# A two-block transformer on one core: gate columns as three products of split parts, gate areas used twice in the expert stage, latent scaling moved

## The reference, cut to what matters

```python
# first block, a layer
x = x + merged @ w_out                       # mixer
x = x + memory_cross_attention(...)
aff = softmax(h @ w_router)                  # 16 experts
gates, idx = top_k(aff.T, cap=32)            # each expert picks 32 tokens
a, u = xs @ w_gate[e], xs @ w_up[e]          # 1024 x 1024 each
y = (silu(a) * u) @ w_down[e] * gates        # added back at idx
# second block, a layer
p = rmsnorm(h) @ w_in                        # its last 2048 columns are gate_a, gate_b
y_a = rwkv7_time_mix(...) @ w_out_rwkv       # a scan over the tokens, done in chunks of 32
y_b = mla(q_lat, kv_lat, k_pe, ...) @ w_out_mla   # q_lat, kv_lat: columns of p, RMS-normed
h = h + (sigmoid(gate_a) * y_a + sigmoid(gate_b) * y_b) @ w_out
h = h + conv_ffn(rmsnorm(h))
```

## Time and profile before

| | us |
|---|---|
| median of 3 runs | 2285.09 |
| range of the 3 runs | 2283.28 to 2287.34 |
| the profiled execution's own time | 2283.18 |
| its span, first to last instruction | 2281.0 |
| PE busy | 2050.3 |
| DVE busy | 872.1 |
| ACT busy | 700.5 |

### The profile page before, as it was taken

The page is one execution under the profiler, slowest core; times in us unless marked ns, Lnnn a source line. Parts: engine busy times, 40 slices in busy tenths (PEclk is TensorE's granted clock), DMA queues, the critical chain, the costliest instruction groups (busy, mean ns, idle before and its releaser), DMA issues.

```text
span 2281.0 us, 38226 instructions
## 1 busy us (share of the span) xinstructions
PE 2050.3 (90%) x16988; PEld 1379.4 (60%) x16988; DVE 872.1 (38%) x1262; ACT 700.5 (31%) x1005; POOL 40.6 (2%) x65
## 2 busy tenths in 40 slices
PE   8999978788779999987778789999999999989998
PEld 6887433333328887333333338565899885658996
DVE  6444111110006444111111127246577472365774
ACT  5544111111115453111111125213444452144443
POOL 1000000000001000000000000000000000000000
PEclk9999898888889998888888889999999999999999
DMA  8246899999996247899999995221754352216540
GB/s 320 93 153 274 329 429 428 429 428 428 429 419 224 74 185 306 358 429 429 428 428 428 429 408 203 77 76 37 236 186 162 131 200 77 71 43 223 185 176 19
DMA packets 139087, 592.28 MB, mean 260 GB/s; under 512 B 5680, under 2 KB 59136, under 8 KB 114384
## 3 DMA queue, kind: packets, MB, share of 16 engines
q1 hardware_dynamic: 137856, 586.67, 65.0%
q0 software_dynamic: 1104, 3.70, 0.4%
HBM read 589.30 MB, written 1.05 MB: 259 GB/s over the span
## 4 chain that ended last, share of the span: by engine, by line
PE 68%; DMA 24%; DVE 3%; issue 2%; ACT 1%; SPq 1%; DVEq 0%; POOLq 0%; ACTq 0%; POOL 0%
PE ps L574 33%; DMA ring<-in_w_up 24%; PE ps L1163 11%; PE ps L2144 5%; PE ps L1984 2%; PE ps L890 2%; PE ps L1130 2%; PE ps L2183 1%; PE ps L1184 1%; PE ps L591 1%; PE ps L989 1%; PE ps L1085 1%; PE ps L1065 1%; DVE ring_lo L550 1%; SPq L781 0%
## 5 line engine op out<-in xcount | busy, mean ns | idle before, releaser
L1163 PE MATMUL ps<-ring,area 128*32 128x512 f32 x1984 | 312.1, 714 | 129.4 <-DMA ring<-in_w_up 129.4
L550 DVE TENSOR_TENSOR ring_lo<-ring,slab_hi 128x2048 fp32r<-128x2048 f32 x136 | 311.4, 2292 | 223.6 <-ACT slab_hi L545 223.4
L545 ACT ACTIVATE slab_hi<-ring 128x2048 fp32r<-128x2048 f32 x136 | 260.0, 1913 | 283.0 <-PE ps L574 265.2
L1163 PEld LDWEIGHTS ps<-ring,area 128*32 128x32 f32 x1984 | 73.2, 128 | 332.6 <-issue 168.1
L574 PE MATMUL ps<-hT_hi,slab_hi 128*128 128x256 f32 x832 | 234.7, 282 | 3.0 <-DVE hT_lo L567 1.5
L574 PE MATMUL ps<-hT_lo,slab_hi 128*128 128x256 f32 x832 | 233.4, 281 | 0.0
L574 PE MATMUL ps<-hT_hi,ring_lo 128*128 128x256 f32 x832 | 232.6, 280 | 0.0
L1749 DVE TENSOR_TENSOR area<-ps,par 128x256 f32<-128x256 f32 x32 | 13.6, 425 | 493.1 <-PE ps L1130 493.1
L1399 ACT ACTIVATE area<-ps 128x512 f32<-128x512 f32 x32 | 19.1, 597 | 552.2 <-PE ps L1163 552.2
L1184 PE MATMUL ps<-ring,area 128*32 128x512 f32 x992 | 160.3, 804 | 29.8 <-DVE area L1769 29.8
L574 PEld LDWEIGHTS ps<-hT_hi,slab_hi 128*128 128x128 f32 x832 | 156.1, 188 | 4.2 <-issue 2.2
(11 more groups left out here) (374 smaller groups left out, 2978.8 us busy)
## 6 DMA issues: line engine op xcount, KB each, us to landing
ring<-in_w_up SPq DMA_DIRECT2D x64, 2048.0 KB, 20.3
ring<-in_w_down SPq DMA_DIRECT2D x62, 2048.0 KB, 21.8
ring<-in_w_gate SPq DMA_DIRECT2D x60, 2048.0 KB, 14.9
ring<-in_w_ffn_up SPq DMA_DIRECT2D x44, 1024.0 KB, 7.8
ring<-in_w_in SPq DMA_DIRECT2D x18, 2048.0 KB, 10.0
ring<-in_w_ffn_down SPq DMA_DIRECT2D x10, 2048.0 KB, 7.8
ring<-in_xattn_w_kv SPq DMA_DIRECT2D x8, 2048.0 KB, 16.9
ring<-in_w_in SPq DMA_DIRECT2D x10, 1024.0 KB, 12.1
```

Source lines behind the costliest of these rows:

```text
L545: return m.nc.scalar.activation(hi, whole, ACT.Copy)
L550: return m.nc.vector.tensor_tensor(lo, whole, hi, ALU.subtract)
L1163: ins = mm(ps[32 * g:32 * g + CAP, 1, :], m.tokT[:, k, :], gate_up[i][:, k % 4, (g % 2) * BANK:(g % 2 + 1) * BANK], start=k == 0, stop=k = ...
```

## The change

1. *Expert stage.* `m.first_gate` is used twice a layer: for expert 0 and then for expert 2. The first halves (rows 0 and 1 of the four) of expert 1's first w_up slab and of expert 2's first w_gate slab are issued as soon as PE has done k = 0 and 1 of expert 0 (`first_rows_used`), the second halves after slot 2 is freed. Expert 2's second w_gate slab follows expert 1's first w_down slab. Slot 3 is freed by the first matmul of `gather` in place of the first transpose behind it.
2. *Gates.* Gate slabs 2 and 3 (32 of 64 steps a layer) become `exact` products: the normed tokens and both slabs are split, five `high` on ACT and five `low` on DVE a layer, each 128x2048. The parts lie in slots 0 and 1, whose gate slabs are used up by then, in the slabs themselves and in a new area `gate_hi`. The order of these steps changes (four k of tile 0, four of tile 1, and so on). Some `GATE_FILLS` in the second half grow by a step, the rest shrinks from seven steps to two.
3. *Ring.* Slots 0 and 1 are freed only at the head of `tensor_mla`. The order of the loads becomes half of w_out (slot 2), w_out_mla, w_out_rwkv, the other half of w_out.
4. *Latent norm.* Its four DVE instructions move in front of the wait for `h_full` in `vector_rwkv`.
5. `Aak` moves into slot 5, AREA grows by 320 columns, `gpsimd_between` waits two experts longer.

```diff
@@ sync_first
-    into_slots(GATE_SLOTS, up_down, 1, 1, 3)
+    up, gate = GATE_SLOTS, m.first_gate
+    sp.wait_ge(*m.at("first_rows_used", l))
+    for rows, loaded in ((slice(0, 2), m.s("second_up_rows_loaded")), (slice(2, 4), m.landed[up])):
+        if rows.start:
+            ring_wait(m, sp, up, l * HELD1_LAYER[up] + 1 + HELD1[up])
+        sp.dma_start(slab(m, up, 4, D)[:, rows], expert("w_up", 1, 0)[:, rows]).then_inc(loaded, 16)
+        sp.dma_start(gate[:, 0][:, rows], expert("w_gate", 2, 0)[:, rows]).then_inc(m.s("third_gate_loaded"), 16)
+    ring_wait(m, sp, up + 1, l * HELD1_LAYER[up + 1] + 1 + HELD1[up + 1])
+    sp.dma_start(slab(m, up + 1, 4, D), expert("w_up", 1, 1)).then_inc(m.landed[up + 1], 16)
+    into_slots(up + 2, ("w_down",), 1, 1, 1)
+    sp.dma_start(gate[:, 1], expert("w_gate", 2, 1)).then_inc(m.s("third_gate_loaded"), 16)
+    into_slots(up, ("w_up",), 2, 2)
     last_down(2)
-    into_slots(0, ("w_gate",), 2, 1)
-    into_slots(GATE_SLOTS, up_down, 2, 2, 3)
-    into_slots(0, ("w_gate",), 3, 2)
+    into_slots(up + 2, ("w_down",), 2, 2, 1)
+    into_slots(0, ("w_gate",), 3, 1)
@@ tensor_experts
+                if behind_up and k == 0 and t == 0:
+                    ins.then_inc(m.free[3], 1)
...
+                if first and k == 1 and g == 3:
+                    ins.then_inc(s("first_rows_used"), 1)
...
-            if c == 0:
+            if last and c == 0:
                 ins.then_inc(m.free[3], 1)
@@ sync_second
+    whole(W_OUT2, "w_out_2", 0)
+    whole(W_OMLA, "w_out_mla_2", 0, k=4, n=D)
     whole(W_ORW, "w_out_rwkv_2", 0, k=4, n=D)
-    whole(W_OMLA, "w_out_mla_2", 0, k=4, n=D)
-    for j in range(2):
-        whole(W_OUT2 + j, "w_out_2", j * BANK)
+    whole(W_OUT2 + 1, "w_out_2", BANK)
@@ tensor_second
-    release.append(W_GATES + PAIRS - 1)
+    release.extend((W_GATES + PAIRS - 1, W_GATES, W_GATES + 1))
@@ _gate_fills
-                     ("whole", 2), ("fourth_wide", 3), ("eighth", 2), ("keys", 3), ("block", 2), ("block_wide", 2), ("cross", 2),
-                     ("close", 2), ("rows", 2), ("wu", 3), ("q", 2), ("g", 1), ("h", 4)):
+                     ("whole", 2), ("fourth_wide", 3), ("eighth", 2), ("keys", 4), ("block", 3), ("block_wide", 2), ("cross", 3),
+                     ("close", 2), ("rows", 3), ("wu", 4), ("q", 2), ("g", 1), ("h", 4)):
...
+EXACT_GATES = 2
+def gate_step(i):
+    j, r = i // (2 * KD), i % (2 * KD)
+    if j < EXACT_GATES:
+        return j, r // KD, r % KD
+    return j, r // 4 % 2, r // KD * 4 + r % 4
...
+def gate_half(m, j, h):
+    slot, half = PLAN2[W_GATES + j].slot, slice(h * (SLAB // 2), (h + 1) * (SLAB // 2))
+    room = m.ring_lo[:, PLAN2[W_GATES + 1].slot]
+    hi = m.gate_hi[:, :] if (j, h) in ((2, 0), (3, 1)) else room[:, 0:SLAB // 2] if j == 2 else room[:, SLAB // 2:]
+    return hi, m.ring_lo[:, slot, half], m.ring[:, slot, half]
@@ fill, in tensor_rwkv
+                if k % 4 == 0 and t == 0:
+                    wait("gate_lo", 2 * (j - EXACT_GATES) + k // 4 + 2)
...
+                first, ins = exact(m, out, rows, w, k == 0, k == KD - 1)
+                if j == PAIRS - 1 and k == 0 and t == 0:
+                    first.then_inc(used(W_GATES + j - 1), 1)
...
-            elif k == 0 and t == 0 and j:
-                ins.then_inc(used(W_GATES + j - 1), 1)
+            elif j == EXACT_GATES and t == 1 and k == 3:
+                ins.then_inc(s("gates_half"), 1)
@@ scalar_rwkv, behind block(1, "D2", 0)
+    wait("gates_full", 2)
+    wait("n1_whole")
+    high(m, *gate_rows_split(m)).then_inc(s("gate_hi"), 1)
+    landed2(m, act, l, W_GATES + 2)
+    high(m, *gate_half(m, 2, 0)).then_inc(s("gate_hi"), 1)
     gate_rows("second_wide")
     block(3, "D", 2)
     gate_rows("fourth_wide")
+    high(m, *gate_half(m, 2, 1)).then_inc(s("gate_hi"), 1)
+    landed2(m, act, l, W_GATES + 3)
+    high(m, *gate_half(m, 3, 0)).then_inc(s("gate_hi"), 1)
     tokens(4, m.ktok)
...
     block(10, "D2T", 1)
+    wait("gates_half")
+    high(m, *gate_half(m, 3, 1)).then_inc(s("gate_hi"), 1)
     gate_rows("close")
@@ vector_rwkv
     chunk_mask("X", 2, "low32x")
+    wait("gate_hi", 1)
+    low(m, *gate_rows_split(m)).then_inc(s("gate_lo"), 1)
...
     wide_mask(3, m.Arb, 0)
+    wait("gate_hi", 2)
+    low(m, *gate_half(m, 2, 0)).then_inc(s("gate_lo"), 1)
...
     tt(M["ID"], bank(2), M["ID"], ALU.add).then_inc(s("inv_d"), 1)
+    for h in range(2):
+        wait("gate_hi", 3 + h)
+        low(m, *gate_half(m, 2 + h, 1 - h)).then_inc(s("gate_lo"), 1)
     wide_mask(5, m.Ark, 0)
...
     tt(M["DT"], bank(2), M["DT"], ALU.add).then_inc(s("inv_d"), 1)
+    wait("gate_hi", 5)
+    low(m, *gate_half(m, 3, 1)).then_inc(s("gate_lo"), 1)
     wait("prod_full", 7)
     chunk_mask("Aak", 4, "up32")
...
+    wait("l_rstd")
+    for t in range(NT):
+        for i, part in enumerate((slice(0, QL), slice(QL, QL + KVL))):
+            c = 74 + 2 * t + i
+            v.tensor_scalar(m.lat[:, t, part], m.lat[:, t, part], m.stat[:, c:c + 1], None, ALU.mult).then_inc(s("l_norm"), 1)
     wait("h_full")
```

More of the change, by code:

```diff
@@ L527, in allocate @@
     m.n1_lo = over("n1_lo", area_at, 16384, KD, T)
+    m.gate_hi = over("gate_hi", area_at, 16704, SLAB // 2)
     m.ident_r, m.causal_r = over("ident_r", area_at, 0, P), over("causal_r", area_at, P, P)
@@ L1131, in gather, with expert @@
                          start=t == 0, stop=t == NT - 1)
+                if behind_up and k == 0 and t == 0:
+                    ins.then_inc(m.free[3], 1)
         ins.then_inc(s("tok_full"), 1)
-    def expert(e, first=False, second=False, last=False):
+    def expert(e, first=False, second=False, third=False, last=False):
         n = e + (l * E + 1)
+        own_gate = first or third
         down = (w[4], m.second_down if second else w[5])
-        gate_up = [m.first_gate[:, i] if first and i < GATE_SLOTS else w[i] for i in range(4)]
+        gate_up = [m.first_gate[:, i] if own_gate and i < GATE_SLOTS else w[i] for i in range(4)]
         def slab_landed(s):
@@ L1200, in tensor_experts @@
     pe.wait_ge(*at("x_perm", l))
-    gather(l * E + 1)
+    gather(l * E + 1, behind_up=False)
     expert(0, first=True)
     expert(1, second=True)
-    with pe.Fori(2, E - 1) as e:
+    expert(2, third=True)
+    with pe.Fori(3, E - 1) as e:
         expert(e)
@@ L2114, with gate_rows_split @@
 _gate_fills()
-def gates_done(point):
-    return GATE_FILLS[point][1] // KD
+EXACT_GATES = 2
[4 more added lines that the diff above has]
+    return j, r // 4 % 2, r // KD * 4 + r % 4
+def gates_done(point):
+    return sum(gate_step(i)[2] == KD - 1 for i in range(GATE_FILLS[point][1]))
+def gate_rows_split(m):
+    room = m.ring_lo[:, PLAN2[W_GATES].slot]
+    return room[:, 0:SLAB // 2], room[:, SLAB // 2:], m.hT[:, :, :].rearrange("p k n -> p (k n)")
+def gate_half(m, j, h):
[3 more added lines that the diff above has]
+    return hi, m.ring_lo[:, slot, half], m.ring[:, slot, half]
 def tensor_rwkv(m, pe, l, landed, used):
@@ L2133, in fill @@
         for i in range(*GATE_FILLS[point]):
-            n, k = i // KD, i % KD
-            j, t = n // 2, n % 2
+            j, t, k = gate_step(i)
+            n = 2 * j + t
+            out, tokens = ps[:, 6 + t, :], slice(t * P, (t + 1) * P)
             if k == 0:
-                if t == 0:
-                    landed(W_GATES + j)
                 if n < 2:
@@ L2142, in fill @@
                     wait("gates_sig", n - 1)
-            w = slab(m, PLAN2[W_GATES + j].slot, KD, BANK)
-            ins = mm(ps[:, 6 + t, :], m.hT[:, k, t * P:(t + 1) * P], w[:, k, :], start=k == 0, stop=k == KD - 1)
+            if j < EXACT_GATES:
+                if k == 0 and t == 0:
+                    landed(W_GATES + j)
+                w = slab(m, PLAN2[W_GATES + j].slot, KD, BANK)
+                ins = mm(out, m.hT[:, k, tokens], w[:, k, :], start=k == 0, stop=k == KD - 1)
+            else:
+                if k % 4 == 0 and t == 0:
+                    wait("gate_lo", 2 * (j - EXACT_GATES) + k // 4 + 2)
+                rows = [a.rearrange("p (k n) -> p k n", n=T)[:, k, tokens] for a in gate_rows_split(m)[:2]]
+                w = [a.rearrange("p (k n) -> p k n", n=BANK)[:, k % 4, :] for a in gate_half(m, j, k // 4)[:2]]
+                first, ins = exact(m, out, rows, w, k == 0, k == KD - 1)
+                if j == PAIRS - 1 and k == 0 and t == 0:
+                    first.then_inc(used(W_GATES + j - 1), 1)
             if k == KD - 1:
                 ins.then_inc(s("gates_full"), 1)
-            elif k == 0 and t == 0 and j:
-                ins.then_inc(used(W_GATES + j - 1), 1)
+            elif j == EXACT_GATES and t == 1 and k == 3:
+                ins.then_inc(s("gates_half"), 1)
     def turn(b, src, half):
```

34 lines of the change are left out of this document (17 added, 17 removed).

## The result

The changed kernel takes 2270.47 us (median of 8 runs, 2263.3 to 2277.33) against 2285.08 us (8 runs) for the kernel before: ratio 0.9939, 95% interval 0.9925 to 0.9952. That is 14.6 us faster. The forecast was 2257.8 us, 27.3 us faster, and the result lies half a microsecond outside the range. The profiled execution took 2271.71 us.

What follows compares the result with a forecast made beforehand. DMA was taken to bound the expert stages and PE the RWKV stages. Terms 10.5 + 11.8 + 5.0 = 27.3 us off the profiled 2283.2 gave 2255.9, plus 1.9 for the median: 2257.8 us, range 2250 to 2270.

Steps and rivals of the forecast that it cites:

- Expert stage: Head of both expert stages: transfers start 1.8 us earlier and flow unbroken; 10.5 us less, bounds 0 to 10.5.
- over 400 GB/s: Sign at the first expert stage's head: the stretch from 244 to 264 us runs at over 400 GB/s.
- a DMA share of 1: Sign at the experts' head: the forecast fails if the DMA share there stays below 1.
- Rival (b): Expert stage gains nothing because the w_down wait in SP's list stops the queue; 2268.3 us, chance 0.05.
- Gate steps: RWKV stages: split products save 0.184 us a step, 32 steps in each of two layers; 11.8 us less.
- rival (d): RWKV fills: split products do not hide their weight loads, so the kernel gets slower; 2293.9 us, chance 0.04.
- Rival (c): RWKV stage: the chain through ACT and DVE becomes the bound and eats the gates' saving; 2269.6 us, chance 0.09.
- The ring's loads: RWKV stages: moving 2 MB transfers behind them removes part of PE's 10.6 us of holes; 5.0 us less.
- The bound of 0: RWKV stages: no gain from the moved loads if holes are tied to the instruction stream or w_out's transfer makes its own.
- rival (a): RWKV stages: PE's holes stay or move with the w_out transfer; 2262.8 us, chance 0.22.

Runs made afterwards that it cites:

- e10_after_192_waits: The kernel after with 192 already satisfied waits in PE's stream of the last expert of layer 1; 2260.88 us, ratio 0.9892.
- e7: The kernel after with 142 already satisfied waits in PE's stream of the last expert of layer 1; 2257.23 us, ratio 0.9882.
- e2: The kernel before with part 1 of the change alone (first gate area used twice, slot 3 freed earlier); 2274.93 us, ratio 0.9962.
- e8: The kernel before with 114 already satisfied waits in PE's stream of the last expert of layer 1; 2286.31 us, ratio 1.0014.
- e4: The kernel after with w_out's transfer held until `tensor_mla` and four `blocks` of each RWKV stage issued twice; 2300.04 us, ratio 1.0067.
- e5: The kernel after with w_out's transfer held until `tensor_mla` and all gate steps in float32, nothing split; 2269.49 us, ratio 0.9944.
- e1: The kernel after with w_out's transfer held until `tensor_mla` begins (slot 2 too freed only there); 2261.57 us, ratio 0.9902.

## Why the prediction was off

**Expert stage, −10.5: right, measured −13.1 in the profiles, of which some 10 are the change's.** The mechanism is as worked out: SP's first issue at 244.46, 20 us at 382 GB/s, the full rate in layer 1. The signs "over 400 GB/s" and a DMA share of 1 were missed in layer 0 (0.94), by the later start: 20 us from 245.07 have 405 GB/s and 0.99. Layer 0 gave 5.9 us (4.9 as the times stand, and 1.1 for the later start), 5.3 predicted. Layer 1 gave 7.2, 5.2 predicted. The rest there came ahead of the transfers: the 32 records of `gather` at the stage's head took 6.61 us at a granted clock of 0.53 before and 3.95 us at 0.93 after. That is chance and no gain, since with the same code up to there e10_after_192_waits has 6.85 us. From the first to the last gate or up product the two stages take 433.5 and 433.6 us before, 428.2 and 429.1 after, 9.8 us less. Rival (b) is refuted: w_down's issue did not stop the queue.

**Gate steps, −11.8: the size is right, but it shows only at a good place.** PE's busy time in the stages falls by 11.4 us from before to e7, by 6.0 in the kernel after, where more of the work behind holes runs at the lower clock. A split product takes 0.232 us, so rival (d) is refuted. No `high` or `low` is waited for: the chain through both stages of the kernel after is PE and "issue" throughout, but for 0.95 us of DVE in the state loop. Rival (c), which is closest in time with 2269.6, has the wrong cause.

**The ring's loads, −5.0, bounds 0 to −10.6: this is the step that failed.** Measured: +6.0 us of idle time and some 5.4 us of work at the lower clock, 11.4 us in the wrong direction. The bound of 0 was "they are tied to the instruction stream", which they are; what I left out is that the change moves the code within that stream. It writes out a third expert ahead of the stages and changes the fills in them, and the pieces of 256 instructions then end at other instructions. The price is paid where two pieces are used up faster than the next comes, and it is highest where that one is due under a 2 MB transfer: rival (a) had that half of it, the hole of 3.96 us under w_out, but with 2262.8 us no growth of the others either. Moved by 71 instructions, the term comes to −3.0 us (idle 13.0 to 10.0 in e7), and the kernel to 2257.2 where 2257.8 was forecast. That this is so near is partly luck, as nothing in the prediction chose that place.

So the kernel after is 27 us faster than before at a good place and 14.6 where it stands. Averaged over the places tried with waits or without (four of before, the six different ones of after, one profile each) the stages take 237.3 and 224.4 us: about 13 us gained in them, where 16.8 were forecast. The place takes these back, since the kernel before stands 2.3 us below its average and the kernel after 10.6 above its own. The best version is the kernel after with 142 waits, 2257.23 us; with w_out's transfer held as well it is the same within the intervals.

What stays open: why the kernel before has its best place where it stands, how long a piece takes from its request, and why e2 is 5 us longer in its stages than e8, though its holes end only nine records from those of e8 (5.09 us in one where e8 has 3.45).

The Trainium skill (Runtime: NRT & Kernel Launch, Instruction fetch mechanics) says that instructions come in sequential blocks of 16 KiB, 256 of them, while the block before is executed, and that the cost is mostly hidden. The blocks agree: 256 more records brought one more packet each time in e4, a shift of 256 gave the same holes, and the holes counted end multiples of 256 records apart. "Mostly hidden" does not hold here: 18.9 us of PE's idle time in 235, and 4.4 us for each added block; the measurement decides.

## What to carry to other kernels

When PE idles with "issue" in straight code, look for the 16 KB packets of the instruction queue, and count the records between two holes: a multiple of 256 gives the cause away. Code of many 32x32 products uses its instructions faster than they come (256 in 1.22 us against one piece in 3.25 us or more), and an edit anywhere ahead, even an unrolled loop two stages earlier, moves the holes. Before a change of under 1% is judged, time it, and the kernel before, at two or three shifts of the code (satisfied waits in a place where the engine is idle anyway do it; 142 cost nothing here, 256 some 5 us); otherwise the place is measured with the change. In such code the saving of a shorter fill may partly come back as a wait (e5 fits this, but doesn't show it), and a large transfer is best kept away from it.

## What the runs showed of the hardware

- Pieces of 16 KB for PE came at best every 3.2 us in this code (start to start, all twenty traces), for 256 records that execute in 1.22 us in `blocks`.
- The 102 holes of 1 us and more end multiples of 256 records apart within their stage, each 1.2 to 1.6 us after a piece has come in.
- With w_out's transfer issued between two pieces they lay 6.6 and 6.8 us apart, and 3.4 and 4.0 us without it (e1).
- Behind 18 of the 24 holes of 2 us and more in the twenty traces the granted clock fell from 1.00 to 0.50 within 6 us (in the kernel after at 1446.50 to 1446.75), behind six it stayed at 1.00; 12 products then take up to 5.49 us in place of 2.78.
- 142 satisfied waits took 13 us off a kernel of 2270; the range over the places was 17.4 us for the kernel after and 6.1 us for the kernel before, by the stages of one profile each. Two profiles at the same place (shifts 0 and 256) differ by 5.5 us.
- Recorded instructions grow by N/2 for N satisfied waits, and the shift is N/2 as well (71 for 142, 256 for 512).
